# GpSimd combines the two probability maps of a differential-attention head

## The chip, the cores and the metric

The kernel runs on one core of a Trainium2 chip. The metric is the device time of one execution in microseconds (us): the median of 3 runs of the kernel before is 3297.37 us (3291.95 to 3299.84).

A core has a matrix engine (TensorE, PE in the rows, with PEld for its weight loads), two elementwise engines (VectorE, DVE; ScalarE, ACT), a third one of eight small processors (GpSimd, POOL), and queues that start DMA transfers (SP). Each engine runs its own instructions in order. Engines wait for each other only through semaphores. GpSimd works in SBUF, the on-chip memory; the score banks of the matrix engine lie in PSUM, which VectorE and ScalarE read.

## The reference, cut to what matters

The model has four layers. Only layer 1 is of the kind touched here, differential attention: per head two score maps, two softmaxes, and their difference weighted by a learned lambda.

```python
lam = _diff_lambda(b_lam[slot], lam_init)
...
def blk(qi):
    s = jnp.einsum('bqhcd,bkhcd->bhcqk', qi, k).astype(F32) * scale
    p = jax.nn.softmax(s, axis=-1)
    a = (p[:, :, 0] - lam * p[:, :, 1]).astype(v.dtype)
    return jnp.einsum('bhqk,bkhe->bqhe', a, v)
...
o = _rms(o, norm_g) * (1.0 - lam_init)
return o.reshape(b, lq, H_B * 2 * DH_B) @ w_out
```

128 context tokens attend to themselves (128 keys); 256 latent tokens attend to themselves and to 128 cached keys (384 keys). There are 8 heads of 128 columns; each of the two maps uses 64 of them. `_rms` over the 128 columns of a head is the head norm.

## The kernel before, in words

The tokens are three tiles of 128. An item is one tile and one head: items 0 to 7 are the context tile (128 keys, "narrow"), items 8 to 23 the two latent tiles (384 keys, "wide"). Four engines run a pipeline over the 24 items, and the order on each engine is written out by the loops below:

- PE, step i (L2272 to L2302): the two score maps of item i (L2281); the transposes of the combined map of item i-2 (L2290), which wait for `prob_done`; the product with the values of item i-3 (L2301), which waits for the copied transpose. Scores of item i also wait until both exponentials of item i-2 are done.
- VectorE, step i (L1706 to L1740): the row maxima of item i (L1711); the reciprocals of the two row sums of item i-1 (L1721) and the ratio that map 1 is to be weighted with (L1722); the scaled output of item i-4 (L1728); the combination of the two maps of item i-1 in one instruction, p0 = p1 * ratio + p0 (L1735).
- ScalarE, step i (L1179 to L1203): the two exponentials of item i with their row sums (L1188), then the copy of the transposed map of item i-2 out of PSUM (L1196).
- GpSimd takes no part in the items. It has one other duty here, the roots of the head norm: `root` (L675) is a small TENSOR_SCALAR (L677), a wait for itself, and a TENSOR_TENSOR with the power -1/2 (L678). `mixer_root` (L705) does it for four pieces, `AT_PIECES`: the 8 heads of tile 0, the 8 of tile 1, and twice 4 heads of tile 2.

For each piece ScalarE squares the outputs (L1176), VectorE sums the squares (`heads_summed`, L1647), GpSimd takes the root, and VectorE scales (`heads_scaled`, L1654). `SUM_AT` = (13, 21, 24) and `SCALE_AT` = (16, 23, 26) say at which VectorE steps the first three pieces are summed and scaled. The fourth is done after the items. The output projection begins with transposes of the scaled heads (L2216), which wait for the scaled third piece.

`steps.settle(ins)` makes an engine wait for its own instruction before the next. At most four items hold a buffer of maps (`PROBS` = 4).

Of the kernel before, what the change touches and what calls it, by code (L numbers as in the profile page):

```python
# [26 lines left out]
P = 128  # L27
# [4 lines left out]
T = TP + TS  # L32
TC = T + 2
NT = T // P
# [4 lines left out]
HEADS = D // P  # L39
# [44 lines left out]
PROBS = 4  # L84
# [56 lines left out]
def build(nc, inp, out, stages=3 * DEPTH):  # L141
# [253 lines left out]
    ratio_done = sem("ratio_done")  # L395
# [266 lines left out]
    def _(pool):  # L662
# [12 lines left out]
        def root(span, mean_of, ready):  # L675

            steps.settle(pool.tensor_scalar(rstd[:, span], sumsq[:, span], 1.0 / mean_of, EPS, ALU.mult, ALU.add))  # L677
            pool.tensor_tensor(rstd[:, span], rstd[:, span], neg_half[:, span], ALU.pow).then_inc(ready, 1)  # L678
# [23 lines left out]
                pool.wait_ge(res_prod, 6 * r)  # L702
            pool.dma_start(gate_bc[:].rearrange("p c d -> p (c d)"), gate_dram.to_broadcast([P, 2 * D])).then_inc(gate_landed, 16)

        def mixer_root():  # L705
            for n, (t, lo, hi) in enumerate(AT_PIECES):
                pool.wait_ge(oss_ready, n + 1)
                root(slice(HEADS * t + lo, HEADS * t + hi), P, orstd_ready)

        def load_means():  # L710

# [3 lines left out]
        def attention(layer):  # L715
            pool.dma_start(past_k[:], inp["past_k"]).then_inc(past_in, 16)
            pool.dma_start(past_v[:], inp["past_v"]).then_inc(past_in, 16)
            pool.wait_ge(qkv_copied, 8 * NT)
            pool.dma_start(out["cache_k"], at_k[:, 0]).then_inc(cache_out, 16)
            pool.dma_start(out["cache_v"], at_v[:, 0]).then_inc(cache_out, 16)  # L720

        def delta_net(layer):
            a = layer // 3
# [99 lines left out]
        for r in range(NORMS):  # L823
            kind = ("ffn", "abca"[r // 3], "ffn")[r % 3]
            if r == 0:
                for t in range(NT):
                    norm_root(0, t)
                pool.dma_start(tri[:], inp["tri"]).then_inc(tables_in, 16)
                pool.dma_start(rope_tab[:], inp["rope_tab"]).then_inc(tables_in, 16)
                pool.dma_start(rows[:], inp["rows"].to_broadcast([P, ROWS])).then_inc(tables_in, 16)  # L830
            if r == 6:
                load_means()
            if kind == "a":
                delta_net(r // 3)
            gate_store(r)
            gate_load(r)
            if kind == "b":
                attention(r // 3)
                mixer_root()
            if r == NORMS - 1:  # L840
                pool.wait_ge(res_prod, 6 * (NORMS - 1))
                pool.dma_start(final_row[:], inp["final_g"].to_broadcast([P, D])).then_inc(final_in, 16)
            residual_roots(r)
# [411 lines left out]
    def _(dve):  # L1255
# [430 lines left out]
        def attention(ph, out_ph):  # L1686
# [19 lines left out]
            for i in range(items + 4):  # L1706
                if i < items:
                    par, slot, keys = i % 2, i % PROBS, P if i < HEADS else T
                    dve.wait_ge(score_done, i + 1)
                    m = at_small[:, AT_NEG_MAX + 2 * slot:AT_NEG_MAX + 2 * slot + 2]  # L1710
                    dve.tensor_reduce(m, banks[:, 4 * par:4 * par + 2, 0:keys], AX.X, ALU.max, negate=True).then_inc(max_done, 1)  # L1711
                if 1 <= i <= items:

                    j = i - 1
                    slot = j % PROBS
                    recip = at_small[:, AT_RECIP + 2 * slot:AT_RECIP + 2 * slot + 2]
                    total = at_small[:, AT_SUM + 2 * slot:AT_SUM + 2 * slot + 2]
                    dve.wait_ge(exp_done, j + 1)
                    if j >= PROBS:
                        dve.wait_ge(ao_copied, j - PROBS + 1)  # L1720
                    steps.settle(dve.reciprocal(recip, total))  # L1721
                    dve.scalar_tensor_tensor(at_small[:, AT_SCALED + slot:AT_SCALED + slot + 1], recip[:, 1:2], neg_lam, total[:, 0:1],  # L1722
                                             ALU.mult, ALU.mult).then_inc(ratio_done, 1)
                if i >= 4:
                    j = i - 4
                    at = AT_RECIP + 2 * (j % PROBS)
                    dve.wait_ge(ao_done, j + 1)
                    dve.tensor_scalar(at_o[:, j // HEADS, j % HEADS], ps[4 * (j % 2) + 3][:, 0:P], at_small[:, at:at + 1], None,  # L1728
                                      ALU.mult).then_inc(ao_copied, 1)
                if 1 <= i <= items:  # L1730
                    j = i - 1
                    slot, keys = j % PROBS, P if j < HEADS else T
                    dve.wait_ge(ratio_done, j + 1)
                    p0, p1 = prob[:, slot, 0, 0:keys], prob[:, slot, 1, 0:keys]
                    dve.scalar_tensor_tensor(p0, p1, at_small[:, AT_SCALED + slot:AT_SCALED + slot + 1], p0,  # L1735
                                             ALU.mult, ALU.add).then_inc(prob_done, 1)
                if i in SUM_AT:
                    heads_summed(SUM_AT.index(i))
                if i in SCALE_AT:
                    heads_scaled(SCALE_AT.index(i))  # L1740
# [765 lines left out]
```

## Time and profile before

| | |
|---|---|
| median of the 3 runs | 3297.37 us |
| the profiled execution's own time | 3295.78 us |
| its span | 3293.7 us |
| PE, DVE, ACT, POOL busy, of the span | 96%, 75%, 41%, 8% |
| mean granted TensorE clock | 0.981 |

The span is the stretch that the trace covers, 2.1 us shorter than the execution's time. Almost all of it is matrix work of the feed-forward blocks and projections (the line of the big matmuls, L1843, makes up 71% of the chain that ended last). The attention core is the stretch from 1373.4 us, when the first scores start, to 1428.3 us, when the transposes for the output projection start: 55 us, 1.7% of the span. It is the only place that the change touches. A share of the whole span therefore says little here. What has to be read is the trace of these 55 us.

### The profile page before, as it was taken

To read this page: it belongs to the slowest core of one execution; us is meant where nothing else is said; L and a number is where in the kernel's file an instruction comes from. 1 tells how busy PE (TensorE), PEld (TensorE's weight loads), DVE (VectorE), ACT (ScalarE), POOL (GpSimd) and SP (SyncE) were. 2 spreads that over 40 slices of the span, in tenths; PEclk is the share of its full clock that TensorE was granted. 3 is DMA by queue.
4 is the path that set the end of the run, shared out by engine and by line. 5 is a ranking of instruction groups with operands and counts; after the bars stand their busy time and mean duration, and the time that the engine had idled before them with its cause. 6 is when DMAs were issued, how large, how long until landed. Compare 5 with 4: busy or idle time off the path is not lost.

```text
span 3293.7 us, 51882 instructions
## 1 busy us (share of the span) xinstructions
PE 3150.6 (96%) x19124; PEld 2922.2 (89%) x19124; DVE 2475.6 (75%) x4250; ACT 1339.0 (41%) x2417; POOL 254.3 (8%) x381
## 2 busy tenths in 40 slices
PE   8998998899999999889999999999999999889997
PEld 6998988889999998769999998899999989888997
DVE  7998866678877884667887887788778887666644
ACT  3333655343343334453334333433433355634332
POOL 1000005400000000010000001000000000450000
PEclk9999999999999999899999999999999999999999
DMA  7654310235544553214554544355445521024332
GB/s 282 232 222 174 118 53 27 79 150 212 208 177 182 219 202 122 84 71 179 203 208 156 213 201 164 150 201 220 168 179 223 198 98 72 14 73 159 146 116 94
DMA packets 66015, 514.80 MB, mean 156 GB/s; under 512 B 8145, under 2 KB 16337, under 8 KB 18145
## 3 DMA queue, kind: packets, MB, share of 16 engines
q1 hardware_dynamic: 60514, 492.08, 38.8%
q0 software_dynamic: 5376, 21.04, 1.7%
q8 instruction: 80, 1.31, 0.2%
q14 instruction: 45, 0.37, 0.0%
HBM read 508.28 MB, written 4.82 MB: 156 GB/s over the span
## 4 chain that ended last, share of the span: by engine, by line
PE 81%; DVE 13%; ACT 2%; issue 2%; DMA 0%; POOL 0%; ACTq 0%; SPq 0%; DVEq 0%; POOLq 0%
PE bank L1843 71%; DVE mod_junk L445 4%; PE bank L2033 3%; DVE split_lo L1264 2%; PE bank L2045 2%; DVE xhat L1414 1%; DVE x L1418 1%; ACT split_hi L867 1%; PE bank L1984 1%; PE bank L2039 1%; DVE hidden L1385 1%; DMA mod_first<-mod_rows 0%; PE bank L1891 0%; DVE xS_lo L1353 0%; PE bank L1892 0%
## 5 line engine op out<-in xcount | busy, mean ns | idle before, releaser
L1843 PE MATMUL bank<-xS_hi,split_hi 128*128 128x386 f32 (+2 forms) x3280 | 1117.3, 341 | 2.9 <-DVE xS_lo L1353 2.0
L1843 PE MATMUL bank<-xS_lo,split_hi 128*128 128x386 f32 (+2 forms) x3280 | 1110.9, 339 | 0.0
L1843 PE MATMUL bank<-xS_hi,split_lo 128*128 128x386 f32 (+2 forms) x3280 | 1109.4, 338 | 0.0
L1264 DVE TENSOR_TENSOR split_lo<-raw,split_hi 128x1024 fp32r<-128x1024 f32 x644 | 780.1, 1218 | 244.6 <-ACT split_hi L867 244.4
L867 ACT ACTIVATE split_hi<-raw 128x1024 fp32r<-128x1024 f32 x644 | 650.9, 1051 | 395.8 <-DMA raw<-ffn_w 266.6
L445 DVE SCALAR_TENSOR_TENSOR mod_junk<-mod_raw,cond 128x1024 f32<-128x1024 f32 x544 | 665.7, 1224 | 54.5 <-DVE mod_junk L445 28.4
L1843 PEld LDWEIGHTS bank<-xS_hi,split_hi 128*128 128x128 f32 (+1 forms) x3280 | 616.9, 188 | 18.3 <-DVE xS_lo L1353 5.3
L1843 PEld LDWEIGHTS bank<-xS_lo,split_hi 128*128 128x128 f32 (+1 forms) x3280 | 618.8, 189 | 9.9 <-issue 0.4
L1843 PEld LDWEIGHTS bank<-xS_hi,split_lo 128*128 128x128 f32 (+1 forms) x3280 | 616.5, 188 | 1.0
L1843 PE MATMUL bank<-split_hi,hid_hi 128*128 128x512 f32 x1056 | 414.2, 392 | 5.1 <-DVE hid_lo L1389 5.1
L1843 PE MATMUL bank<-split_lo,hid_hi 128*128 128x512 f32 x1056 | 412.8, 391 | 0.0
L1843 PE MATMUL bank<-split_hi,hid_lo 128*128 128x512 f32 x1056 | 412.2, 390 | 0.0
L962 ACT ACTIVATE silu_g<-gate_n 128x128 f32<-128x128 f32 x352 | 141.5, 449 | 648.4 <-DVE gate_n L1377 648.4
L1843 PEld LDWEIGHTS bank<-split_hi,hid_lo 128*128 128x128 f32 x1056 | 198.8, 188 | 43.1
L1843 PEld LDWEIGHTS bank<-split_hi,hid_hi 128*128 128x128 f32 x1056 | 198.8, 188 | 43.0 <-DVE hid_lo L1389 7.4
L967 ACT ACTIVATE hid_hi<-hidden 128x384 fp32r<-128x384 f32 x176 | 92.5, 526 | 344.6 <-DVE hidden L1385 344.6
L1843 PEld LDWEIGHTS bank<-split_lo,hid_hi 128*128 128x128 f32 x1056 | 198.8, 188 | 35.3
L1389 DVE TENSOR_TENSOR hid_lo<-hidden,hid_hi 128x384 fp32r<-128x384 f32 x176 | 98.4, 559 | 109.1 <-ACT hid_hi L967 109.1
L696 POOL DMA_DIRECT2D gate_dram<-gate_turned x48 | 24.3, 511 | 1830.6 <-DVE gate_turned L1296 1830.5
L1843 PE MATMUL bank<-split_hi,xS_hi 128*128 128x384 f32 (+2 forms) x360 | 135.4, 376 | 17.9 <-DVE xS_lo L1670 7.8
L1381 DVE TENSOR_TENSOR up_n<-bank,rstd_bc 128x386 f32<-128x386 f32 x176 | 97.5, 554 | 72.3 <-PE bank L1843 72.3
L1433 DVE SCALAR_TENSOR_TENSOR scratch<-scratch,cols 128x193 f32<-128x193 f32 x384 | 131.2, 416 | 14.4 <-ACT scratch L992 14.4
(277 smaller groups left out, 3043.3 us busy)
## 6 DMA issues: line engine op xcount, KB each, us to landing
raw<-ffn_w SPq DMA_DIRECT2D x175, 1536.0 KB, 7.5
mod_raw<-mod_w SPq DMA_DIRECT2D x136, 1024.0 KB, 4.8
raw<-a_in_w SPq DMA_DIRECT2D x20, 1536.0 KB, 6.3
gate_bc<-gate_dram POOLq DMA_DIRECT2D x12, 1024.0 KB, 4.9
raw<-b_in_w SPq DMA_DIRECT2D x8, 1536.0 KB, 6.4
raw<-a_out_w SPq DMA_DIRECT2D x4, 1536.0 KB, 7.6
mod_first<-mod_w SPq DMA_DIRECT2D x4, 1024.0 KB, 14.9
mod_first<-mod_rows SPq DMA_DIRECT2D x4, 1024.0 KB, 17.6
```

Of the source, the lines that this page charges most:

```text
L445: eng.scalar_tensor_tensor(mod_junk[:], weights[:, t], 1.0, cond[:, c], ALU.mult, ALU.mult, accum_out=mod_column(m, t, c)).then_inc(mod_co ...
L867: act.activation(split_hi[:, unit.slot, q, 0:w], raw[:, unit.slot, q, 0:w], ACT.Copy).then_inc(hi_ready, 1)
L962: ins = act.activation(silu_g[:, par, lo:hi], gate_n[:, par, lo:hi], ACT.Silu, bias=gate_n[:, par, T + c:T + c + 1])
L967: act.activation(hid_hi[:, par], hidden[:, par], ACT.Copy).then_inc(hid_hi_done, 1)
L1264: dve.tensor_tensor(split_lo[:, unit.slot, q, 0:w], raw[:, unit.slot, q, 0:w], f32(split_hi[:, unit.slot, q, 0:w]), ALU.subtract).then_inc ...
L1381: dve.tensor_tensor(up_n[:, par], ps[up_bank][:, 0:TC], rstd_bc[:], ALU.mult).then_inc(up_norm, 1)
L1385: ins = dve.scalar_tensor_tensor(hidden[:, par, lo:hi], up_n[:, par, lo:hi], up_n[:, par, T + c:T + c + 1], silu_g[:, par, lo:hi], ALU.add ...
L1389: dve.tensor_tensor(hid_lo[:, par], hidden[:, par], f32(hid_hi[:, par]), ALU.subtract).then_inc(hid_done, 1)
L1433: dve.scalar_tensor_tensor(dst, src, weight, dst, ALU.mult, ALU.add).then_inc(conv_step, 1)
L1843: ins = pe.matmul(out, lhsT, rhs, start=start and i == 0, stop=stop and i == 2)
L2033: ins = pe.matmul(ps[bank][:, h * P:(h + 1) * P], lhsT(h), rhs(h), start=True, stop=True)
L2045: ins = pe.matmul(ps[bank][half, h * HALF:(h + 1) * HALF], lhsT(half, h), rhs(half, h), start=True, stop=True)
```

## The change

The combination p0 = p1 * ratio + p0 goes from VectorE (one instruction per item) to GpSimd (two per item, with a wait for itself between them): p1 = p1 * ratio, then p0 = p0 + p1. The semaphore that PE waits for, `prob_done`, now comes from GpSimd. Since GpSimd's queue now holds the items, the four head-norm roots, which stood in one piece behind the cache stores, are placed between its items: behind the items 12, 20 and 23 (j + 1 in `SUM_AT`) and at the end.

```diff
-        def mixer_root():
-            for n, (t, lo, hi) in enumerate(AT_PIECES):
-                pool.wait_ge(oss_ready, n + 1)
-                root(slice(HEADS * t + lo, HEADS * t + hi), P, orstd_ready)
+        def mixer_root(n):
+            t, lo, hi = AT_PIECES[n]
+            pool.wait_ge(oss_ready, n + 1)
+            root(slice(HEADS * t + lo, HEADS * t + hi), P, orstd_ready)
...
             pool.dma_start(out["cache_v"], at_v[:, 0]).then_inc(cache_out, 16)
+            for j in range(NT * HEADS):
+                slot, keys = j % PROBS, P if j < HEADS else T
+                pool.wait_ge(ratio_done, j + 1)
+                p0, p1 = prob[:, slot, 0, 0:keys], prob[:, slot, 1, 0:keys]
+                steps.settle(pool.tensor_scalar(p1, p1, at_small[:, AT_SCALED + slot:AT_SCALED + slot + 1], None, ALU.mult))
+                pool.tensor_tensor(p0, p0, p1, ALU.add).then_inc(prob_done, 1)
+                if j + 1 in SUM_AT:
+                    mixer_root(SUM_AT.index(j + 1))
+            mixer_root(3)
...
                 attention(r // 3)
-                mixer_root()
...
-                if 1 <= i <= items:
-                    j = i - 1
-                    slot, keys = j % PROBS, P if j < HEADS else T
-                    dve.wait_ge(ratio_done, j + 1)
-                    p0, p1 = prob[:, slot, 0, 0:keys], prob[:, slot, 1, 0:keys]
-                    dve.scalar_tensor_tensor(p0, p1, at_small[:, AT_SCALED + slot:AT_SCALED + slot + 1], p0,
-                                             ALU.mult, ALU.add).then_inc(prob_done, 1)
```

GpSimd's rows around the first root, before: the cache stores are followed by the roots at once (L677 and L678 are the two instructions of a root).

```order
L719 DMA out_cache_k<-at_k 128x1024
L720 DMA out_cache_v<-at_v 128x1024
L677 TENSOR_SCALAR rstd<-sumsq 128x8
L678 TENSOR_TENSOR rstd<-rstd,neg_half 128x8
L677 TENSOR_SCALAR rstd<-sumsq 128x8
L678 TENSOR_TENSOR rstd<-rstd,neg_half 128x8
```

GpSimd's rows around the first root, of the change: L725 and L726 are the two new instructions, here of the items 11, 12, 13 and 14.

```order
L725 TENSOR_SCALAR prob<-prob,at_small 128x384
L726 TENSOR_TENSOR prob<-prob 128x384
L725 TENSOR_SCALAR prob<-prob,at_small 128x384
L726 TENSOR_TENSOR prob<-prob 128x384
L677 TENSOR_SCALAR rstd<-sumsq 128x8
L678 TENSOR_TENSOR rstd<-rstd,neg_half 128x8
L725 TENSOR_SCALAR prob<-prob,at_small 128x384
L726 TENSOR_TENSOR prob<-prob 128x384
L725 TENSOR_SCALAR prob<-prob,at_small 128x384
```

The first root now stands between the combinations of the items 12 and 13.

VectorE's rows at the same place, before: the last rows of step 13, the sum of squares, and step 14.

```order
L1728 TENSOR_SCALAR at_o<-bank,at_small 128x128
L1735 SCALAR_TENSOR_TENSOR prob<-prob,at_small 128x384
L1647 TENSOR_REDUCE sumsq<-sq_tmp 128x8
L1711 TENSOR_REDUCE at_small<-bank 128x2
L1721 RECIPROCAL at_small<-at_small 128x2
L1722 SCALAR_TENSOR_TENSOR at_small<-at_small 128x1
L1728 TENSOR_SCALAR at_o<-bank,at_small 128x128
L1735 SCALAR_TENSOR_TENSOR prob<-prob,at_small 128x384
```

The same rows of the change (its lines are 8 higher).

```order
L1736 TENSOR_SCALAR at_o<-bank,at_small 128x128
L1655 TENSOR_REDUCE sumsq<-sq_tmp 128x8
L1719 TENSOR_REDUCE at_small<-bank 128x2
L1729 RECIPROCAL at_small<-at_small 128x2
L1730 SCALAR_TENSOR_TENSOR at_small<-at_small 128x1
L1736 TENSOR_SCALAR at_o<-bank,at_small 128x128
```

Only the combination is gone; the rest stands as it stood. PE and ScalarE keep their order.

## Rows read from the trace of the kernel before

**Rows 1.** Waits, 1374 to 1428.5 us: who waited for whom, us, times, longest.

```profile
PEld bank L2290 <- DVE prob L1735: 15.6, 22, 1.4
```

**Rows 2.** Windows: length, busy (x instructions) of PE, PEld, DVE, ACT, POOL, PEclk, DMA, GB/s.

```profile
1378.00:1382.00 4.00, 4.00 (x20) 2.74 (x18) 2.74 (x11) 2.47 (x14) 0.00 (x0) 0.50 0.00 0
...
1397.00:1426.00 29.00, 25.04 (x150) 15.65 (x149) 27.29 (x64) 20.47 (x60) 3.71 (x4) 1.00 0.00 1
```

**Rows 3.** Timeline, one turn of the wide items: start us, us, engine, line, instruction.

```profile
1409.17 0.95 DVE L1711 TENSOR_REDUCE at_small<-bank 128x2 f32<-128x768 f32 x1
...
1410.16 0.58 ACT L1188 ACTIVATE prob<-bank,at_small 128x384 f32<-128x384 f32 x1 [0.37 <-DVE at_small L1711]
...
1411.29 0.49 ACT L1196 ACTIVATE probT<-bank 128x384 f32<-128x384 f32 x1
1411.56 0.31 PEld L2290 LDWEIGHTS bank<-ident,prob 128*128 128x128 f32 x3 [0.55 <-DVE prob L1735]
...
1411.67 0.96 DVE L1711 TENSOR_REDUCE at_small<-bank 128x2 f32<-128x768 f32 x1 [0.43 <-PE bank L2281]
1411.84 0.53 PEld L2301 LDWEIGHTS bank<-at_v,probT 128*128 128x128 f32 x4
...
1412.71 0.92 PE L2281 MATMUL bank<-kT,qT 64*128 64x384 f32 x4
1412.74 0.22 DVE L1722 SCALAR_TENSOR_TENSOR at_small<-at_small 128x1 f32<-128x1 f32 x1
...
1413.13 0.61 DVE L1735 SCALAR_TENSOR_TENSOR prob<-prob,at_small 128x384 f32<-128x384 f32 x1
...
1413.67 0.96 DVE L1711 TENSOR_REDUCE at_small<-bank 128x2 f32<-128x768 f32 x1
...
1413.80 0.55 PE L2290 MATMUL bank<-ident,prob 128*128 128x128 f32 x3 [0.18 <-DVE prob L1735]
```

**Rows 4.** GpSimd's groups by form, whole trace: busy us, mean ns of one.

```profile
L770 POOL TENSOR_TENSOR att<-att,kq_copy 128x512 f32<-128x512 f32 x24 | 29.7, 1284 | 0.2
L745 POOL COPY blocks<-amap 32x128 f32<-32x128 f32 x64 | 25.7, 401 | 15.0 <-DVE amap L1535 10.2
...
L777 POOL TENSOR_TENSOR att<-dn_v,dn_small 128x512 f32<-128x512 f32 x16 | 16.2, 1050 | 3.9 <-PE bank L2033 3.9
...
L730 POOL MEMSET halves<- 128x384 f32 x2 | 0.8, 415 | 4.2 <-DMA dn_const<-dn_const 4.2
```

**Rows 5.** Timeline, the first root and its neighbours on VectorE.

```profile
1398.46 1.21 DVE L1647 TENSOR_REDUCE sumsq<-sq_tmp 128x8 f32<-128x1024 f32 x1
...
1399.77 0.20 POOL L677 TENSOR_SCALAR rstd<-sumsq 128x8 f32<-128x8 f32 x1 [32.34 <-DVE sumsq L1647]
...
1400.06 1.67 POOL L678 TENSOR_TENSOR rstd<-rstd,neg_half 128x8 f32<-128x8 f32 x1
...
1401.05 0.61 DVE L1735 SCALAR_TENSOR_TENSOR prob<-prob,at_small 128x384 f32<-128x384 f32 x1
```

**Rows 6.** Timeline, a narrow item at the lower clock.

```profile
1381.14 0.22 DVE L1722 SCALAR_TENSOR_TENSOR at_small<-at_small 128x1 f32<-128x1 f32 x1
...
1381.54 0.34 DVE L1735 SCALAR_TENSOR_TENSOR prob<-prob,at_small 128x128 f32<-128x128 f32 x1
...
1382.06 0.47 PE L2290 MATMUL bank<-ident,prob 128*128 128x128 f32 x1
```

**Rows 7.** Timeline, transposes of items 8, 20 and 23, and the end of the core.

```profile
1390.01 0.55 PE L2290 MATMUL bank<-ident,prob 128*128 128x128 f32 x3
...
1418.29 0.55 PE L2290 MATMUL bank<-ident,prob 128*128 128x128 f32 x3 [0.17 <-DVE prob L1735]
...
1425.63 0.55 PE L2290 MATMUL bank<-ident,prob 128*128 128x128 f32 x3 [0.78 <-DVE prob L1735]
...
1426.54 1.01 POOL L678 TENSOR_TENSOR rstd<-rstd,neg_half 128x4 f32<-128x4 f32 x1
...
1428.33 0.88 PE L2216 MATMUL bank<-ident,at_o 128*128 128x128 f32 x6 [0.64 <-DVE at_o L1654]
```

## The prediction, made before the changed kernel was run

> **What bounds the kernel now.** I read the page first, for the place of the change: the attention core is 55 of 3294 us, and the chain that ended last runs through it. Then the waits of this stretch. PE's weight loads for the transposes waited 15.6 us for VectorE's combination, in 22 of 24 items [rows 1], and by the windows VectorE is busy 27.29 of 29 us in the wide stage and PE 25.04 [rows 2]. That looks as if VectorE were the bound and any instruction taken off it a gain. The timeline says otherwise, because it shows what each engine waits for in turn.
>
> In the wide stage two loops close after two items each, and every step of them can be read in [rows 3]. The first runs through ScalarE: maxima at 1409.17, exponentials at 1410.16 (0.99 later), copy of a transposed map at 1411.29 (1.13), product with the values at 1411.84 (0.55), scores at 1412.71 (0.87), the next maxima but one at 1413.67 (0.96). That is 4.50 us for two items, 2.25 each. No combination is in it. The second runs through the combination: transposes at 1411.56, product 1411.84 (0.28), scores 1412.71 (0.87), maxima 1413.67 (0.96), ratio after the maxima 1.07 (1411.67 to 1412.74), combination 0.39 behind the ratio (1412.74 to 1413.13), next transposes 0.67 behind that (1413.13 to 1413.80). Sum 4.24 us for two items. So the first loop sets the pace now and the second has 0.26 us to spare. VectorE's own turn without a wait is 2.00 us (1411.67 to 1413.67), PE's about 2.0 as well (0.28 + 0.87 + a score of some 0.87).
>
> **The change part by part.** *Taken from VectorE:* the combination, 0.54 us of its turn (1413.13 to 1413.67), in 24 items. Since the ScalarE loop of 4.50 us doesn't hold it, this alone gives next to nothing in the steady state. It does give room for the sums and scalings of 1.21 us [rows 5], which now stretch the turns they stand in.
>
> *Added on GpSimd:* per item a handover from VectorE, TENSOR_SCALAR, the wait for itself, TENSOR_TENSOR. The handover is 0.10 us (the sum of squares ends at 1399.67, GpSimd starts at 1399.77) and the self-wait 0.09 (1399.97 to 1400.06) [rows 5]. Neither new instruction is in the trace. TENSOR_TENSOR over 128x384: the nearest row is L770, in place with a second tensor, 1.284 us for 512 elements [rows 4]. Three quarters of it, 0.96, is the lower end, the whole 1.28 the upper. With 0.20 us of fixed cost (TENSOR_SCALAR of 8 elements, [rows 5]) it is 0.20 + 0.75 x 1.08 = 1.01; I take that. TENSOR_SCALAR over 128x384 reads one tensor. Lower end: MEMSET of the same size, 0.415 us, which reads none. Above it: L777, which reads one tensor and a broadcast value, 1.050 x 3/4 = 0.79; far above, three times the copy of 128 elements, 3 x 0.401 = 1.20 [rows 4]. I take 0.60, the MEMSET and the fixed 0.20 of an instruction that reads, as it is the row of the same size. For 128 elements the same gives 0.20 + 1.08/4 = 0.47 (0.32 to 0.67) and 0.30 (0.20 to 0.40).
>
> [Rows 4] have 2.1 ns per element above the fixed cost where two tensors are read. The Trainium skill, GPSIMD Engine Reference, section 3.1, gives 2.6 cycles per element at 1.2 GHz for two inputs, which agrees; section 4.1 calls one input roughly line rate, which no row shows. By that page TENSOR_SCALAR would be an estimated 0.2 + 0.32 = 0.52 us instead of 0.60, and the sum below 0.9 us smaller.
>
> *The wide loop then:* transposes, product 0.28, scores 0.87, maxima 0.96, ratio 1.07, its duration 0.22, handover 0.10, 0.60, 0.09, 1.01, handover to PE 0.06 (1413.74 to 1413.80 is the like). Sum 5.26 us for two items, 2.63 each, against 2.25. The combination now lasts 1.80 us from the end of the ratio where it took 0.78 (1412.96 to 1413.74). What hid it, the 0.26 us, is gone, and this loop takes the lead from the ScalarE loop.
>
> *Narrow items, 0 to 7.* PE is at half clock (0.50, full busy, [rows 2]). From the end of the ratio to the combined map 0.52 us now (1381.36 to 1381.88), and the transposes start 0.18 behind, of which 0.06 is the handover: 0.12 to spare [rows 6]. Then 0.10 + 0.30 + 0.09 + 0.47 = 0.96. So 0.96 - 0.52 - 0.12 = 0.32 per pair, for six items 1.0. The first item pays 0.96 - 0.38 (0.34 and what lies around it) = 0.58 with nothing before it, the first wide one the difference of the two lengthenings, 1.02 - 0.44 = 0.58. Item 8 is transposed some 2.1 us later.
>
> *The roots.* Behind item 12 stand 0.10 + 0.20 + 0.09 + 1.67 = 2.06 us [rows 5] before item 13's 1.70 can start: 3.76 us from transposes to transposes instead of 2.63. Item 14 comes 1.75 behind that, at 5.51 instead of 5.26, so 0.25 remain for its whole line of every second item. The other line, late by 1.1, is pushed on, but item 20 stands in the first one. Items 8 to 20: 12 x 2.63 + 0.25 = 31.81 us, before 28.28 (1390.01 to 1418.29, [rows 7]): +3.5. Items 20 to 23: root 2.06 and three combinations on a GpSimd that never waits, 3.76 + 1.75 + 1.75 = 7.26, before 7.34: -0.1. VectorE's sums of 1.21 cost nothing in this count: its turn is 1.46 + 1.21 = 2.67 where it has to make one, about the 2.63 of the loop.
>
> *The end.* Item 23's transposes to the output projection's take 2.70 us now (1425.63 to 1428.33). The root of 4 heads (0.20 + 0.09 + 1.01) now follows the combination directly, since its sum has long been there, and 0.78 us for scaling and start follow it (1427.55 to 1428.33): about 2.06. -0.6.
>
> Sum: +2.1 + 3.5 - 0.1 - 0.6 = +4.9 us. The output projection behind the core starts that much later with the same work, so the whole of it reaches the end. No DMA is moved past anything: GpSimd's next DMA comes only with the next sub-layer. Against the profiled execution's 3295.78 us it is 3300.7; that execution lies 1.6 below the median, so for a median I say 3297.37 + 4.9 = 3302.3.
>
> Both instructions together enter the sum about 11 times (12/2 in the loop, once at item 8, once behind the first root, three times at the end). At the lower ends, 0.415 + 0.96, it is 2.6 us less: +2.3. At 0.79 + 1.28, with the narrow ones also dearer, 5.1 + 0.8 more: +10.8. At the far end 1.20 + 1.28 it would be +15.
>
> **The rivals.** What a measurement of this kernel can tell from no change is about 0.2%, 6.6 us.
>
> *GpSimd's instructions cost their upper rows* (0.79 and 1.28). The place is the loop from ratio to transposes, and it decides for "slower" from 0.60 + 1.01 + 0.15 = 1.76 us for the two. For it: no row shows a TENSOR_SCALAR with a tensor behind it, and it needs a per-partition factor. Against: MEMSET moves the same bytes in 0.415. Time 3297.4 + 10.8 = 3308.2.
>
> *VectorE and GpSimd shut each other out.* During the first root's 1.67 us VectorE ran a combination that reads two tensors in SBUF, 0.61 us as everywhere else [rows 3, 5]: nothing was held up. But that root reads 8 elements per partition, and the new instructions read 384. Price: VectorE's ratio or scaling held, or holding GpSimd, for up to a root's 1.67 us at each of the two roots, 3.3 more: +8.2, 3305.6. The Trainium skill, SBUF — State Buffer, section "Who interferes with whom", states such a rule, an exclusive lock between a VectorE instruction with two SBUF inputs and a GpSimd one that reads SBUF. [Rows 5] don't show it; by the rule 3305.6, without it 3302.3.
>
> *VectorE was the bound after all.* If the waits of [rows 1] are the cause and GpSimd's longer way is absorbed by the four map buffers, PE's 2.0 us per item is what remains: 16 x 0.24 = -3.9, 3293.5. Against it speaks the first loop of [rows 3], without any combination. Even this is inside 0.2%.
>
> *The clock.* PE's granted clock was 0.50 in the narrow stage and 1.00 in the wide one, where PE is 86% busy [rows 2]. With 2.0 us of work in 2.63 it is 76%. Should it fall once to the lower of its two levels (1.2 of 2.4 GHz), an item's PE work doubles to 4.0 us; two items in such a spell cost 2 x 1.4 = 2.8: +7.7, 3305.1.
>
> **How the numbers follow.** The forecast gets 0.55, the dear instructions 0.25, the lock 0.08, VectorE the bound 0.07, the clock 0.05. Slower by over 0.2% are the second, third and fifth: 0.38. Within 0.2% the first and fourth, less 0.03 for a set of runs that scatters to the other side (they spread over 7.9 us before): 0.59. Faster 0.03. The time is that of the likeliest case, 3302.3. Its own range is 3299.7 to 3304 (+2.3 to +6.6). The range for 8 in 10 takes in the dear instructions and a little of the scatter: 3297 to 3310.
>
> **What would show it.** Right: the two new groups on GpSimd at 0.5 to 0.7 and 0.95 to 1.1 us; wide transposes 2.6 us apart, 3.7 at item 13 and at item 21; PE's wait for the combined map now at GpSimd and longer than 15.6 us; VectorE with idle time before its maxima. The rest of the kernel unmoved. Wrong: transposes still 2.25 apart or nearer (the loop is not what I think), GpSimd instructions outside their ends, VectorE's ratio longer than 0.22 us next to GpSimd work, or a clock of 0.50 after 1390 us.

## The result, and the profile after

The change makes the kernel slower: 3316.02 us against 3296.88 in the same comparison (medians of 6 runs each), ratio 1.0054, 95% interval 1.0043 to 1.0064. That is some 18 us where I had forecast 4.9, with 3310 as the upper end of my range. One of the six runs took 4881.94 us at a mean granted clock of 0.593 and is left out of the ratio; the median of the other five is 3314.74. The profiled execution took 3314.74 us (before 3295.78), its span is 3312.6 us (before 3293.7).

All of the loss is in the attention core. In the trace of after the first maxima start at 1373.94 us (before 1373.97), the transposes of the output projection at 1447.93 (before 1428.33): 73.99 us against 54.36, +19.6 (the spans differ by 18.9; everything else together is 0.7 shorter). In what follows T0, T8 and T23 are the starts of the transposes of these items. All lengths are read from the timelines.

| us | T0 after the first maxima | T0 to T8 | T8 to T20 | T20 to T23 | T23 to the output projection | core |
|---|---|---|---|---|---|---|
| before | 2.16 | 13.88 | 28.28 | 7.34 | 2.70 | 54.36 |
| after | 3.03 | 17.21 | 40.56 | 9.93 | 3.26 | 73.99 |

The page of the profile has the new work on GpSimd, 302.0 us busy where it was 254.3; VectorE is down by 9 us only (2466.7 for 2475.6).

The groups by form of the core (busy us, mean ns of one | idle before) give the prices:

```profile
L725 POOL TENSOR_SCALAR prob<-prob,at_small 128x384 f32<-128x384 f32 x16 | 22.0, 1373 | 10.8 <-DVE at_small L1730 10.5
L726 POOL TENSOR_TENSOR prob<-prob 128x384 f32<-128x384 f32 x16 | 15.9, 994 | 1.3
...
L725 POOL TENSOR_SCALAR prob<-prob,at_small 128x128 f32<-128x128 f32 x8 | 4.8, 606 | 14.1 <-DVE at_small L1730 14.1
L726 POOL TENSOR_TENSOR prob<-prob 128x128 f32<-128x128 f32 x8 | 3.6, 453 | 0.7
```

TENSOR_TENSOR costs what I took (0.99 for 1.01, 0.45 for 0.47). TENSOR_SCALAR costs twice as much: 1.37 on average and about 1.25 undisturbed, for 0.60; 0.61 for 0.30. It is dearer than the instruction that reads two tensors.

The waits of 1370 to 1450 us (us, times, longest) answer to [rows 1]:

```profile
PEld bank L2291 <- POOL prob L726: 32.8, 23, 3.2
...
DVE at_small L1719 <- PE bank L2282: 28.7, 20, 4.5
```

PE waits twice as long for a combined map as before, and VectorE, which had next to no idle time in the wide stage, now waits for scores. The timeline of two undisturbed items (to be read against [rows 3]) has the loop as I had drawn it:

```profile
1425.81 0.55 PE L2291 MATMUL bank<-ident,prob 128*128 128x128 f32 x3 [0.75 <-POOL prob L726]
1426.09 0.53 PEld L2302 LDWEIGHTS bank<-at_v,probT 128*128 128x128 f32 x4
...
1426.96 0.92 PE L2282 MATMUL bank<-kT,qT 64*128 64x384 f32 x4
...
1427.92 0.96 DVE L1719 TENSOR_REDUCE at_small<-bank 128x2 f32<-128x768 f32 x1 [1.27 <-PE bank L2282]
...
1428.87 0.55 PE L2291 MATMUL bank<-ident,prob 128*128 128x128 f32 x3 [0.99 <-POOL prob L726]
1428.99 0.22 DVE L1730 SCALAR_TENSOR_TENSOR at_small<-at_small 128x1 f32<-128x1 f32 x1
...
1429.31 1.25 POOL L725 TENSOR_SCALAR prob<-prob,at_small 128x384 f32<-128x384 f32 x1 [0.49 <-DVE at_small L1730]
...
1430.63 1.00 POOL L726 TENSOR_TENSOR prob<-prob 128x384 f32<-128x384 f32 x1
...
1431.68 0.33 PE L2291 MATMUL bank<-ident,prob 128*128 128x128 f32 x1 [0.76 <-POOL prob L726]
```

Transposes at 1425.81, product 0.28 later, scores 0.87, maxima 0.96, ratio 1.07, then 0.32 to GpSimd, 1.25, 0.07, 1.00, 0.05 to the next transposes but one at 1431.68: 5.87 us for two items. My sum with the measured durations in it, 3.65 + 1.245 + 0.99, gives 5.89.

Two things come on top. The windows (length, busy of PE, PEld, DVE, ACT, POOL, granted clock, DMA, GB/s) show the lower clock not only in the narrow stage:

```profile
1392.00:1394.00 2.00, 0.09 (x2) 0.00 (x0) 1.83 (x3) 1.69 (x7) 1.92 (x2) 0.89 0.00 0
1394.00:1399.00 5.00, 4.82 (x18) 3.43 (x18) 1.91 (x6) 1.73 (x6) 2.84 (x4) 0.50 0.00 0
1409.00:1411.50 2.50, 0.22 (x2) 0.22 (x3) 1.51 (x4) 1.42 (x5) 2.42 (x3) 1.00 0.00 0
1416.00:1418.00 2.00, 0.00 (x0) 0.00 (x0) 1.49 (x5) 1.03 (x4) 1.92 (x2) 0.86 0.00 0
1418.00:1424.00 6.00, 5.76 (x22) 4.28 (x22) 1.51 (x4) 1.66 (x6) 2.97 (x4) 0.50 0.01 3
1424.00:1438.00 14.00, 9.31 (x57) 5.72 (x56) 8.29 (x20) 8.22 (x25) 11.51 (x11) 0.99 0.00 1
1440.00:1442.00 2.00, 0.32 (x3) 0.13 (x2) 1.41 (x5) 0.69 (x2) 1.92 (x2) 0.84 0.00 0
1442.00:1444.00 2.00, 1.63 (x8) 1.63 (x9) 0.00 (x0) 0.49 (x1) 1.92 (x3) 0.50 0.00 0
```

Before, the clock was 1.00 from 1397 to 1426 [rows 2]. Now it is 0.50, the lower of its two levels (1.2 of 2.4 GHz), in three spells: from 1394 to 1400, from 1418 to 1424 and from about 1441.5 to 1448. Each begins behind a stretch in which PE had next to nothing to do (0.09, 0.00 and 0.32 us of work in the 2 us before it). Such a stretch is not enough by itself: from 1409.0 to 1411.5 PE worked 0.22 us, and the clock stayed at 1.00. At the upper level PE is busy 9.31 of 14 us, 66%, where it was 86%, and inside these 14 us the clock did not fall; so no busy share is read from these rows as the cause.

The other is the length of instructions of GpSimd and VectorE that lie beside each other (three places; POOL and DVE rows of the timeline; L1662 is VectorE's head-norm scaling):

```profile
1393.13 0.99 POOL L726 TENSOR_TENSOR prob<-prob 128x384 f32<-128x384 f32 x1
1393.20 0.94 DVE L1730 SCALAR_TENSOR_TENSOR at_small<-at_small 128x1 f32<-128x1 f32 x1
...
1414.78 2.32 POOL L725 TENSOR_SCALAR prob<-prob,at_small 128x384 f32<-128x384 f32 x1 [1.25 <-DVE at_small L1730]
1414.86 1.22 DVE L1662 TENSOR_TENSOR at_o<-at_o,rstd 128x1024 f32<-128x1024 f32 x1
...
1438.06 0.99 POOL L726 TENSOR_TENSOR prob<-prob 128x384 f32<-128x384 f32 x1
...
1438.31 1.82 DVE L1662 TENSOR_TENSOR at_o<-at_o,rstd 128x1024 f32<-128x1024 f32 x1
1439.03 2.21 POOL L725 TENSOR_SCALAR prob<-prob,at_small 128x384 f32<-128x384 f32 x1
```

A TENSOR_SCALAR of 1.25 takes 2.32 and 2.21 us, a scaling of 1.22 takes 1.82, and a ratio of 0.22 takes 0.94 and ends at 1394.14, when GpSimd's addition ends at 1394.12. One engine is held up by the other; this is called the lock below. Which of the two is held can't be told from the starts: at 1414.78 GpSimd's row begins 0.08 us ahead of the scaling, and it is GpSimd that is held (1.07 us), while the scaling takes its usual 1.22.

So the theory for the runs: +19.6 is the loop with dear instructions, the lock, and the clock. Rivals: the two instructions are not the cause but the handover to a third engine is; VectorE or the inserted sums and scalings set the pace; the form of TENSOR_SCALAR matters less than its per-partition factor.

### The profile page after: what moved, and what is told of

Its sections match the earlier page's. It is cut to its first block, busy times and chain, and to the rows that moved or that the text cites. A ratio compares the mean times of both kernels' runs of the same rounds, so it can differ in the third digit from the quotient of the medians.

```text
span 3312.6 us, 51906 instructions
## 1 busy us (share of the span) xinstructions
PE 3156.8 (95%) x19124; PEld 2928.6 (88%) x19124; DVE 2466.7 (74%) x4226; ACT 1342.1 (41%) x2417; POOL 302.0 (9%) x429
## 4 chain that ended last, share of the span: by engine, by line
PE 81%; DVE 12%; ACT 2%; issue 2%; POOL 1%; DMA 1%; ACTq 0%; SPq 0%; DVEq 0%; POOLq 0%
PE bank L1844 71%; DVE mod_junk L445 3%; PE bank L2034 3%; DVE split_lo L1272 2%; PE bank L2046 2%; DVE xhat L1422 1%; DVE x L1426 1%; ACT split_hi L875 1%; PE bank L1985 1%; PE bank L2040 1%; POOL prob L725 0%; DVE hidden L1393 0%; DMA mod_first<-mod_rows 0%; PE bank L1892 0%; POOL rstd L678 0%
## 6 DMA issues: line engine op xcount, KB each, us to landing
mod_first<-mod_w SPq DMA_DIRECT2D x4, 1024.0 KB, 14.9
```

## The experiments

The times below are medians, with the ratio to the kernel before in the same comparison (its medians there are 3294.37 to 3296.88), or single executions where so marked. "Filled" is after with unread matmuls on PE, "before, filled" the kernel before with some. The traces of the core are what the verdicts rest on, since single terms are 0.5 to 8 us.

| us | T0 | T0 to T8 | T8 to T23 | T23 to end | core | time, ratio |
|---|---|---|---|---|---|---|
| before | 2.16 | 13.88 | 35.62 | 2.70 | 54.36 | |
| after | 3.03 | 17.21 | 50.49 | 3.26 | 73.99 | 3316.02, 1.0054 [1.0043, 1.0064] |
| no combination | 1.77 | 13.95 | 33.28 | 2.59 | 51.59 | 3292.49, 0.9991 [0.9982, 1.0001] |
| addition only | 2.31 | 14.73 | 35.87 | 2.27 | 55.18 | 3293.54, 0.9999 [0.9989, 1.0008] |
| broadcast factor | 2.78 | 16.38 | 43.44 | 2.91 | 65.51 | 3304.91, 1.0029 [1.0019, 1.0040] |
| filled | 3.18 | 16.19 | 47.19 | 2.62 | 69.18 | 3309.86, 1.0042 [1.0027, 1.0056] |
| filled, small scalings | 3.17 | 16.18 | 45.16 | 2.27 | 66.78 | 3307.83 (single) |
| filled, constant factor | 3.10 | 16.10 | 45.02 | 2.26 | 66.48 | 3305.69 (single) |
| relay, short | 2.33 | 13.91 | 35.63 | 2.54 | 54.41 | 3293.49 (single) |
| relay, long | 2.65 | 15.65 | 36.69 | 2.27 | 57.26 | 3300.14 (single) |
| before, much filled | 5.24 | 11.98 | 35.63 | 2.70 | 55.55 | 3298.20, 1.0009 [1.0000, 1.0018] |
| before, filled | 2.17 | 11.45 | 35.62 | 2.70 | 51.94 | 3291.17, 0.9987 [0.9978, 0.9996] |
| the same, scalings on GpSimd | 2.17 | 11.45 | 34.82 | 2.70 | 51.14 | 3291.98, 0.9987 [0.9978, 0.9996] |

### No combination at all

The combination is left out on every engine, so map 1 never enters the output.

```diff
-            act.wait_ge(prob_done, items)
+            act.wait_ge(ratio_done, items)
...
-                    dve.scalar_tensor_tensor(p0, p1, ..., p0, ALU.mult, ALU.add).then_inc(prob_done, 1)
...
-                    pe.wait_ge(prob_done, j + 1)
+                    pe.wait_ge(ratio_done, j + 1)
```

> The kernel before with the combination of the two maps left out altogether (PE transposes map 0 as it is, as soon as the ratio is there). Loop theory: two loops of two items each set the pace; the one through ScalarE (4.50 us, no combination in it) stays, so wide transposes stay 2.25 us apart where nothing is inserted; only the turns with a sum or a scaling of 1.2 us get shorter, some 2 us in all: about 3294 to 3295. Rival (VectorE is the bound, any instruction taken off it is a gain): transposes 2.0 us apart, core 4 to 6 us shorter, about 3291 to 3293.

Measured: wide transposes pairwise 4.49 us apart, as with the combination. These are the first and the last of three transposes in a row:

```profile
1413.16 0.55 PE L2283 MATMUL bank<-ident,prob 128*128 128x128 f32 x3
...
1417.65 0.55 PE L2283 MATMUL bank<-ident,prob 128*128 128x128 f32 x3
```

So the ScalarE loop of 4.50 us sets the pace of before, and taking the combination off VectorE can't win more than the 2.8 us of core that this kernel shows (2.3 of them from T8 to T23, in the turns with a sum or scaling). VectorE as the bound falls, by the rows: the time alone, 3292.49 beside 3294.68, lies in the range that the rival had named.

### Addition only

The multiplication is left out of after: `-steps.settle(pool.tensor_scalar(p1, p1, at_small[...], None, ALU.mult))`. The ratio is then never applied.

> The change with its first GpSimd instruction (map 1 times ratio) left out; the addition stays on GpSimd. Loop theory: 3.65 + 0.99 - 0.09 = 4.55 us for two items, as good as the 4.50 of the ScalarE loop: transposes 2.25 to 2.3 apart, PE busy enough to keep its clock, time within 2 us of the kernel before. Rival (the loss of the change comes with GpSimd taking part at all: the shared access to SBUF, the roots between the items, the clock): still 5 us or more slower than before.

```profile
1410.97 0.55 PE L2290 MATMUL bank<-ident,prob 128*128 128x128 f32 x3
...
1415.50 0.55 PE L2290 MATMUL bank<-ident,prob 128*128 128x128 f32 x3
```

A pair takes 4.53 us and the time is that of before. Handover, the roots between the items and the addition together cost 0.8 us of core; the other 18.8 come with the multiplication (its own length and what follows from it: no clock of 0.50 behind 1388 us and no ratio over 0.22 us in this trace).

### The relay: VectorE combines, GpSimd only passes on

After with VectorE's combination put back; GpSimd waits for it and does a MEMSET of unread memory before it signals.

```diff
-                steps.settle(pool.tensor_scalar(p1, p1, at_small[...], None, ALU.mult))
-                pool.tensor_tensor(p0, p0, p1, ALU.add).then_inc(prob_done, 1)
-                pool.wait_ge(ratio_done, j + 1)
+                pool.wait_ge(combined, j + 1)
+                if j:
+                    pool.wait_ge(prob_done, j)
+                pool.memset(relay_pad[:, 0:8], 0.0).then_inc(prob_done, 1)     # long: 0:384
```

> VectorE combines the maps as in the kernel before, but PE waits for GpSimd, which waits for VectorE and writes 8 elements of an unused tile per item (MEMSET, about 0.1 us); the roots stand between the items as in the change. Loop theory: the loop through the combination was 4.24 us for two items and gets 0.10 for the handover and 0.10: 4.44, still under the 4.50 of the ScalarE loop, so undisturbed pairs stay at 4.5 us; core 55 to 57 us (the roots stand in the way). Rival (there is no slack: PE waits for the combination, so each 0.2 us of delay counts): pairs of 4.7 us.

> The same with a MEMSET of 384 elements per item (0.415 us). Loop theory: 4.24 + 0.10 + 0.42 = 4.76 us for an undisturbed pair, 0.26 more than now; core some 3 us longer than with the short one. Rival (GpSimd's way is hidden by the four map buffers, only its busy time counts, which is far below an item's 2.25 us): pairs of 4.5 us, as with the short one.

```profile
L727 POOL MEMSET relay_pad<- 128x8 f32 x24 | 2.5, 104 | 49.9 <-DVE prob L1744 49.8
```

```profile
L727 POOL MEMSET relay_pad<- 128x384 f32 x24 | 10.0, 418 | 46.1 <-DVE prob L1744 46.1
...
1412.14 0.55 PE L2299 MATMUL bank<-ident,prob 128*128 128x128 f32 x3 [1.05 <-POOL relay_pad L727]
...
1416.86 0.55 PE L2299 MATMUL bank<-ident,prob 128*128 128x128 f32 x3 [0.66 <-POOL relay_pad L727]
```

With 0.104 us put in, pairs stay at 4.49 (1409.90 to 1414.39): the step fits in the slack of 0.26. With 0.418 they take 4.72 (1412.14 to 1416.86): the slack is used up and the rest is paid in full. The forecast of a loop with a small reserve holds at both sides of it. The handover to a third engine as such costs nothing: the core with the short relay is 54.41 us, less than the 55 to 57 expected, since the roots did not stand in the way.

### A broadcast operand in place of TENSOR_SCALAR

```diff
-                steps.settle(pool.tensor_scalar(p1, p1, at_small[...], None, ALU.mult))
+                ratio = at_small[:, AT_SCALED + slot:AT_SCALED + slot + 1].to_broadcast([P, keys])
+                steps.settle(pool.tensor_tensor(p1, p1, ratio, ALU.mult))
```

> The change with the first GpSimd instruction as a TENSOR_TENSOR whose second operand is the ratio, broadcast over the row, instead of a TENSOR_SCALAR with the ratio as its factor; the result is the same. Loop theory: by the row of the like form (1.050 us for 512 elements) 0.8 us instead of 1.24; undisturbed pairs of items 3.65 + 0.8 + 0.99 = 5.4 instead of 5.87 us, 5 to 6 us less in all, more if the clock stays up: 3305 to 3310. Rival (the two-tensor read costs as much as the scalar form, so TENSOR_SCALAR is not dear as a form but GpSimd is slow here for every form): no gain, 3313 to 3317.

```profile
L726 POOL TENSOR_TENSOR prob<-prob,at_small 128x384 f32<-128x384 f32 x16 | 13.2, 826 | 10.7 <-DVE at_small L1731 10.3
```

The same product in another form takes 0.826 us, pairs are 5.43 apart (3.65 + 0.83 + 0.99 = 5.47), and the core is 8.5 us shorter than after, more than the 5 to 6 expected: the clock is at 0.50 for some 3 us of the wide stage behind 1394 and some 3 us at its end, where after has three spells of 6 to 7. The lock is still there (VectorE's ratio takes up to 0.76 us, the addition 1.85 twice). The kernel is still slower than before.

### PE filled: what the clock costs

After, with four matmuls per step behind the scores whose result nobody reads.

```diff
+                    for _ in range(4):
+                        pe.matmul(ps[4 * par + 2][:, T:T + P], qT[half, h, t * P:(t + 1) * P], kT[half, h, 0:P], start=True, stop=True)
```

> The change with four more matmuls of 128 columns behind the scores of each item, into columns that nobody reads; they stand where PE otherwise waits for the combined map. Clock theory: a part of the loss is PE's clock at 0.50 in three spells of the wide stage; with PE busier the clock stays at 1.00 there and the core is 3 to 5 us shorter than the change's: 3310 to 3312. Rival (the clock spells cost nothing since PE waits for GpSimd anyway): the same or slower than the change, 3315 or more.

```profile
1418.00:1424.00 6.00, 5.97 (x44) 4.87 (x46) 3.02 (x8) 2.93 (x10) 4.15 (x5) 1.00 0.02 4
1424.00:1438.00 14.00, 11.48 (x84) 9.20 (x82) 10.18 (x22) 8.32 (x23) 12.18 (x12) 1.00 0.00 1
...
1440.00:1442.00 2.00, 1.89 (x10) 1.59 (x9) 0.35 (x1) 0.39 (x1) 1.75 (x4) 0.50 0.00 0
```

The granted clock is 1.00 up to 1438, in the narrow stage too; the last spell is left, shorter (0.66 from 1438 to 1440, 0.50 to 1442). Pairs without a disturbance still take 5.87, and the core is 4.8 us shorter: 4.81 is what the lower clock up to there cost in after, 3.30 of it from T8 to T23. The extra matmuls may themselves cost a little. (By the times alone, 1.0042 and 1.0054 with overlapping intervals, it would not be shown; the traces show it.)

### Filled, and the scalings cut to one column: what the lock costs

For the first two pieces VectorE scales one column in 128; the other 127 of each head stay unscaled.

```diff
+            if n < 2:
+                dve.tensor_tensor(at_o[:, t, lo:hi, 0:1], at_o[:, t, lo:hi, 0:1], r[:, :, 0:1], ALU.mult).then_inc(ohat_ready, 1)
+            else:
+                dve.tensor_tensor(at_o[:, t, lo:hi], at_o[:, t, lo:hi], r, ALU.mult).then_inc(ohat_ready, 1)
```

> The change with four more matmuls per item (the clock then stays at 1.00) and with the two scalings of 8 heads reduced to one column per head, 8 elements instead of 1024; to be read against the same kernel with the full scalings (core 69.7 us). Lock theory: two GpSimd multiplications of 2.2 to 2.3 us and VectorE's scaling of 1.82 us come from the two engines shutting each other out of SBUF; all multiplications are 1.25 us now and the core is 1.5 to 2.5 us shorter. Rival (the long ones are GpSimd's own scatter, or wait for something else): still some of 2 us, core less than 1 us shorter.

```profile
L725 POOL TENSOR_SCALAR prob<-prob,at_small 128x384 f32<-128x384 f32 x16 | 19.9, 1245 | 7.4 <-DVE at_small L1733 7.2
```

Now every one of the sixteen takes 1.25 us (longest 1.273), where the filled kernel's mean was 1.372. Two intervals got shorter by 1.05 (item 15) and 0.96 (item 22), and the core by 2.40 (from 69.18, which is the filled kernel's core, and not the 69.7 of the expectation). 2.03 of them lie between T8 and T23. The other 0.37 are nearly all at the end (2.27 for 2.62 us), where the clock is now 1.00 from 1440 to 1442: the last spell of the lower clock went away together with the hold at item 22. What is left of the lock here is small: VectorE's ratio takes up to 0.43 us, and one scaling of 8 elements 0.77.

That it is the hold, and not VectorE's shorter scaling, that gives these 2 us is seen in the next kernel, where the scalings are whole.

### Filled, with a constant in place of the ratio

`pool.tensor_scalar(p1, p1, 0.5, None, ALU.mult)`: map 1 is halved in place of weighted.

> The change with PE's clock held by four more matmuls per item, and the multiplication on GpSimd by the constant 0.5 instead of the ratio of each partition (so the ratio is left out). It asks what makes the TENSOR_SCALAR dear. If the factor that is read per partition does: about 0.6 us for 384 elements, pairs of 4.6 us. If the form itself does: 1.24 us as before, pairs of 5.9 us, core as with the ratio.

```profile
L725 POOL TENSOR_SCALAR prob<-prob 128x384 f32<-128x384 f32 x16 | 18.7, 1168 | 8.0 <-DVE at_small L1730 7.7
L725 POOL TENSOR_SCALAR prob<-prob 128x128 f32<-128x128 f32 x8 | 4.2, 529 | 13.8 <-DVE at_small L1730 13.7
```

Undisturbed, the per-partition factor costs under 0.1 us (1.245 for 1.168); the form costs the rest. But the core is 66.48 us, 2.70 below the filled kernel, and not "as with the ratio": the factor's kind decides over the lock. No multiplication is held any more (longest 1.178 us), with the scaling whole and lying right beside it:

```profile
1412.45 1.17 POOL L725 TENSOR_SCALAR prob<-prob 128x384 f32<-128x384 f32 x1 [1.33 <-DVE at_small L1730]
1412.54 1.49 DVE L1662 TENSOR_TENSOR at_o<-at_o,rstd 128x1024 f32<-128x1024 f32 x1
1413.70 1.18 POOL L726 TENSOR_TENSOR prob<-prob 128x384 f32<-128x384 f32 x1
```

With the ratio the same neighbours took 2.32 and 1.22 us; with a constant the two run side by side for 1.08 us and lose at most 0.27 (1.49 for 1.22), and the addition behind loses 0.19. VectorE's ratio is still held by the addition (up to 1.05 us). The intervals of the items 15 and 22 are 0.98 and 0.72 us shorter than in the filled kernel. Why the constant form is spared no run shows.

### The kernel before, filled

If idle PE time costs clock, before should win in its narrow stage. Matmuls of the identity with itself, unread: first 8 behind each of the first two scores, 2 behind each later one, 6 ahead of the first, 10 behind the output projection's first transposes.

> The kernel before with PE's idle time around the narrow items filled by matmuls of 128 columns that nobody reads: 6 ahead of the first scores, 8 behind each of the first two, 2 behind the others of the context tile, 10 ahead of the output projection. Clock theory: the spell at 0.50 from 1377 to 1386 us goes away, and the one at 1431: core 2 to 4 us shorter, 1 us more behind it, some 3291 to 3293 beside 3295 to 3297 before. Rival (the spell lies beside waits for VectorE and ScalarE, or the extra matmuls stand in the way as much): no change.

A miss. T0 to T8 fell by 1.9 us, but the 8 fillers behind the first scores (16 records from 1370.69 on) took 2.05 us ahead of work that was ready, and T0 came 3.1 us late. So with fewer:

```diff
+                    for _ in range(0 if i == 0 else 3 if i == 1 else 1 if i < HEADS else 0):
+                        pe.matmul(ps[4 * par + 2][:, T:T + P], ident[:], ident[:], start=True, stop=True)
```

with 3 ahead of the first scores and 5 behind those transposes.

> The kernel before with fewer of the unread matmuls: 3 ahead of the first scores, none behind the first, 3 behind the second, 1 behind the others of the context tile, 5 ahead of the output projection; 0.25 us each at full clock, so that they fit into the waits. Clock theory: T0 is no later than before (2.2 us after the first maxima), the clock stays at 1.00, core 2 to 3 us shorter than before's 54.4, 3 to 4 us with the projection's start: 3291 to 3292 beside 3294 to 3295. Rival: the clock falls all the same, or the extra work stands in the way: no gain.

```profile
1378.00:1382.00 4.00, 4.00 (x28) 2.80 (x28) 3.51 (x15) 3.08 (x16) 0.00 (x0) 1.00 0.01 2
...
1430.00:1434.00 4.00, 4.00 (x21) 3.27 (x20) 2.27 (x3) 1.11 (x2) 0.00 (x0) 1.00 0.36 68
```

The clock is 1.00 where it was 0.50 [rows 2]; T0 to T8 takes 11.45 us instead of 13.88. The output projection gives 1.6 more (from its first transposes to the next sub-layer's first root 39.97 us, before 41.54). It beats both kernels: 0.9987, [0.9978, 0.9996], 4 us less than before.

### The same, with the scalings on GpSimd

GpSimd, which is idle in before, takes over the first two scalings, to give VectorE the 1.22 us of each back.

```diff
+                if n < 2:
+                    pool.wait_ge(orstd_ready, n + 1)
+                    r = rstd[:, HEADS * t + lo:HEADS * t + hi].rearrange("p (h o) -> p h o", o=1).to_broadcast([P, hi - lo, P])
+                    pool.tensor_tensor(at_o[:, t, lo:hi], at_o[:, t, lo:hi], r, ALU.mult).then_inc(ohat_ready, 1)
...
-                if i in SCALE_AT:
+                if i == SCALE_AT[2]:
```

> The same, and the two scalings of 8 heads (1.22 us each on VectorE, in the turns of items 16 and 23) on GpSimd behind their roots, where they take 1.9 us and nobody waits for them. Loop theory: 0.9 us less at each of two items, unless the lock takes it back. Lock theory: VectorE's combination (0.61 us, two tensors in SBUF) falls on GpSimd's 1.9 us and is held up once or twice for up to 1.9 us: the combination shows durations of over 1 us, the gain of 1.7 us is gone or turned over.

```profile
1395.24 1.90 POOL L712 TENSOR_TENSOR at_o<-at_o,rstd 128x1024 f32<-128x1024 f32 x1
1396.06 1.09 DVE L1726 SCALAR_TENSOR_TENSOR at_small<-at_small 128x1 f32<-128x1 f32 x1
...
1414.37 1.90 POOL L712 TENSOR_TENSOR at_o<-at_o,rstd 128x1024 f32<-128x1024 f32 x1
1415.23 1.05 DVE L1726 SCALAR_TENSOR_TENSOR at_small<-at_small 128x1 f32<-128x1 f32 x1
```

VectorE's ratio, 0.22 us elsewhere, takes 1.09 and ends at 1397.15, when GpSimd's instruction ends at 1397.14 (the rows' starts and lengths). It takes 1.05 the second time. The combination, of which the expectation said it, is never held (0.61 us); it is the ratio. The core is 0.8 us shorter, half of the 1.7 of the loop theory, and the time is the same. Here the lock is seen by itself: an instruction over one element per partition waits until GpSimd is done.

## Why the prediction was wrong, step by step

**The loops: right.** Without any combination, with the addition alone, with two sizes of relay, with the broadcast form and in after itself a pair takes 4.49, 4.53, 4.49 and 4.72, 5.43 and 5.87 us. All follow from 4.50 for the one loop and 4.24, plus what is added, for the other. That PE waited 15.6 us for VectorE [rows 1] was no sign of VectorE as the bound.

**The price of TENSOR_SCALAR: the step that failed.** I took 0.60 from MEMSET and a fixed 0.20, "as it is the row of the same size". It is 1.245. My far end, three times the copy of [rows 4], was 1.20, right to 4%, but by luck: with the fixed 0.20 taken off first, as I did it for TENSOR_TENSOR, the same row gives 0.20 + 3 x 0.20 = 0.80, and for 128 elements its 0.401 stands against 0.604. I priced the far end (+15) and then ended the range well below it. With the measured sizes the two instructions are 2.235 us instead of 1.61: 0.62 x 11 = 6.9; the narrow ones 1.06 instead of 0.77, three times (four of them, less the one that the first wide item makes good), 0.9. So the sum would have been 4.9 + 7.8 = +12.7. The filled kernel with small scalings, which has no lower clock and next to no lock, measures 66.78 - 54.36 = +12.4.

The other 7.2 of the 19.6 are two terms that my sum put at nothing, the lock and the clock, each with a small chance of its own.

| step | forecast | after | filled, small scalings |
|---|---|---|---|
| up to item 8 | +2.1 | +4.2 | +3.3 |
| items 8 to 23 | +3.4 | +14.9 | +9.5 |
| the end | -0.6 | +0.6 | -0.4 |
| sum | +4.9 | +19.6 | +12.4 |

Its base is the kernel before, whose own narrow stage is at the lower clock; against before filled it is 66.78 - 51.94 = +14.8 at the upper clock in both.

**What the page made of the same price.** The Trainium skill, GPSIMD Engine Reference, section 4.1, I quoted as the view by which TENSOR_SCALAR would be cheaper still (one input at roughly line rate). The rows say the opposite: 1.245 and 0.604 us for 384 and 128 elements are 2.5 ns per element, against (0.99 - 0.45) / 256 = 2.1 for two tensors. With a constant, which leaves one input, it is 2.5 as well ((1.168 - 0.529) / 256). The measurement decides.

**The lock: dismissed wrongly.** I gave it 0.08, since the root of [rows 5] held nothing up. That root reads 8 elements. Instructions of 384 elements and more do hold and are held: 1.25 becomes 2.32 and 2.21, 0.22 becomes 0.94 and, beside 1024 elements, 1.09. The section "Who interferes with whom" of the Trainium skill's page SBUF — State Buffer, which I had quoted for it, agrees with these rows, but not with two others. The root and the multiplication by a constant read SBUF too, and the root held VectorE's combination for nothing, while the multiplication by a constant and the scaling beside it lost 0.27 us at most. There the measurement decides. The cost is 2.40 us, of which 2.0 are the two holds themselves; my 3.3 was not far off, though the partners are mostly the scalings and not the roots.

**The clock: dismissed wrongly.** I gave it 0.05, at 76% of PE's time in use. With the real loop PE is 66% busy, the clock fell three times in the wide stage, and its lower level cost 4.8 us in all, where I had 2.8 for one spell. But the kernel before pays for the lower clock as well, 54.36 - 51.94 = 2.4 us in its narrow stage. At the upper clock in both, the change costs 69.18 - 51.94 = +17.2, so the clock's share in the +19.6 is 2.4 (the filled kernel still has its short last spell).

**And they add up.** Each rival was priced alone and given a chance of its own. All three were true together: 12.4 + 2.4 + 4.8 = 19.6. That this comes out is no check, since the three are successive differences of the same four times; the check is +12.7 from the sum against +12.4. Against the kernel before at the upper clock the parts are 14.8 for the instructions, 2.4 for the lock and 2.4 for the clock. They are not independent. Two of the three spells follow at once on the holds at items 15 and 22, which left PE idle for 2.59 and 2.05 us, and in the filled kernels the last spell is gone when the hold before it is. That the longer loop, with less work for PE in it, brings the first spell fits with the addition-only kernel, which has none, but no run shows it by itself.

**The roots: right in kind.** The first root pushes item 13 out in after:

```profile
1405.85 0.99 POOL L726 TENSOR_TENSOR prob<-prob 128x384 f32<-128x384 f32 x1
...
1406.93 0.20 POOL L677 TENSOR_SCALAR rstd<-sumsq 128x8 f32<-128x8 f32 x1
1407.22 1.68 POOL L678 TENSOR_TENSOR rstd<-rstd,neg_half 128x8 f32<-128x8 f32 x1
1408.91 1.24 POOL L725 TENSOR_SCALAR prob<-prob,at_small 128x384 f32<-128x384 f32 x1
1410.24 0.99 POOL L726 TENSOR_TENSOR prob<-prob 128x384 f32<-128x384 f32 x1
1411.28 0.55 PE L2291 MATMUL bank<-ident,prob 128*128 128x128 f32 x3 [2.32 <-POOL prob L726]
```

Combined map to combined map 4.39 us (1406.84 to 1411.23); I had 3.76, and the 0.64 that TENSOR_SCALAR costs more makes 4.40. The addition-only kernel, where the roots stand at the same places, shows that they cost next to nothing when the items' own work is short (T8 to T23 35.87 for 35.62). The end, for which I had -0.6, came out at +0.6 in after and at -0.4 at the upper clock without the holds: the root did follow at once, and it was the last spell of the lower clock that took the gain back.

**VectorE's relief gives next to nothing:** right; 2.8 us of core at most.

## What to carry to other kernels

Find the loops that close over several engines and write each as a sum of steps; the difference between the longest and the one that is changed is all that a change may cost for nothing (0.26 us here), and the idle time of an engine or its wait doesn't tell it. An instruction whose form no row shows has no price yet: the row of the same size gave 0.60 here, the rows nearest in form 0.79 and 0.80, and it took 1.245. Where the ends that one can name are twofold apart, the range must hold both. When a change lengthens a loop, add up what can follow from it, the lower clock and the time under a lock, instead of giving each a small chance of its own.

## What the runs showed of the hardware that I had not expected

- GpSimd multiplies 128x384 by one value per partition in 1.245 us as TENSOR_SCALAR, 1.17 with a constant, and in 0.826 us as TENSOR_TENSOR with a broadcast operand. For 128 elements it is 0.604, 0.529 and 0.398.
- A VectorE instruction over one element per partition can take 1.09 us instead of 0.22 when GpSimd is inside an instruction over 1024. The root power over 8 elements, 1.67 us long, held nothing up [rows 5].
- A multiplication on GpSimd with a per-partition factor was held for the whole of VectorE's scaling beside it (2.32 us for 1.25). With a constant factor both ran side by side (1.17 and 1.49 us).
- PE's clock fell three times in the wide stage of after, each time behind some 2 us in which PE had almost no work, and it didn't fall behind another such stretch (1409.0 to 1411.5). Unread matmuls in idle PE time brought it back in both kernels (4.8 us in after; 2.4 and 1.6 us in before). Only the last spell stayed, shorter, and went away with the hold before it. How much of the 4.8 belongs to each of the spells isn't separated beyond the 3.30 us between T8 and T23.
